# Attention in steps of two units instead of one, with the output products spread anew over the steps

## What is computed

```python
pa, pb, pc, pd = jnp.split(hl @ w_in, COL_SPLITS, axis=-1)
oa = window_attention_sink(qa, ka, va, kac, vac, a_sink, scale64)
ob = dense_attention(qb, cat(kbc, kb), cat(vbc, vb), scale_b)
oc = diff_combine(dense_attention(qc, cat(kcc, kc), cat(vcc, vc), scale_c), c_lambda, c_subln, layer)
od = dense_attention(qd, cat(kdc, kd), cat(vdc, vd), scale64)
out_lat = jnp.concatenate([merge_heads(oa), merge_heads(ob), oc, merge_heads(od)], axis=-1) @ w_out
```

## Time and profile before

| | |
|---|---|
| median of 3 runs | 2156.08 us (2155.17 to 2156.92) |
| the profiled execution, span | 2157.7 us |
| TensorE matmul busy | 1970.7 us, 91% of the span |
| VectorE busy | 676.9 us, 31% |
| ScalarE busy | 529.7 us, 25% |
| GpSimd busy | 156.9 us, 7% |

### The profile page before, as it was taken

The page is one execution under the profiler, slowest core; times in us unless marked ns, Lnnn a source line. Parts: engine busy times, 40 slices in busy tenths (PEclk is TensorE's granted clock), DMA queues, the critical chain, the costliest instruction groups (busy, mean ns, idle before and its releaser), DMA issues. The chain is left out here.

```text
span 2157.7 us, 27259 instructions
## 1 busy us (share of the span) xinstructions
PE 1970.7 (91%) x10878; PEld 931.5 (43%) x10878; DVE 676.9 (31%) x1753; ACT 529.7 (25%) x1220; POOL 156.9 (7%) x155
## 2 busy tenths in 40 slices
PE   5999989999979999999999899889996898887875
PEld 2436465555633332323323556465554333333322
DVE  3322345666650100101001632366666011110203
ACT  3211154565531000100100321166553010000001
POOL 1100010000010010020100201100000000000000
PEclk8999979999989999999999999999998899999998
DMA  9742020000189999999999302110008899999995
GB/s 352 287 161 81 0 79 1 1 2 1 40 322 414 425 365 418 380 391 419 363 414 420 137 20 78 23 57 1 1 1 342 361 427 426 427 426 427 427 427 213
DMA packets 90935, 515.66 MB, mean 239 GB/s; under 512 B 10594, under 2 KB 15628, under 8 KB 36540
## 3 DMA queue, kind: packets, MB, share of 16 engines
q1 hardware_dynamic: 84496, 493.29, 56.4%
q0 software_dynamic: 4416, 15.21, 2.4%
q10 hardware_dynamic: 1900, 5.43, 0.6%
HBM read 498.69 MB, written 15.20 MB: 238 GB/s over the span
## 5 line engine op out<-in xcount | busy, mean ns | idle before, releaser
L712 PE MATMUL psS<-arena 128*64 128x512 f32 (+9 forms) x4552 | 1136.0, 556 | 70.8 <-DMA arena<-in_w_up 23.1
L712 PEld LDWEIGHTS psS<-arena 128*64 128x64 f32 (+4 forms) x4552 | 450.0, 158 | 666.2 <-issue 585.1
L715 PE MATMUL psT<-ident,arena 128*128 128x128 f32 (+1 forms) x1036 | 171.6, 289 | 47.3 <-DVE arena L2053 13.2
L1930 DVE TENSOR_REDUCE mx<-psS 128x1 f32<-128x768 f32 (+2 forms) x200 | 165.5, 827 | 152.1 <-PE psS L712 150.4
L1281 ACT ACTIVATE arena<-psT 128x768 f32<-128x768 f32 (+7 forms) x261 | 150.3, 577 | 244.0 <-PE psT L715 230.3
L1281 ACT ACTIVATE arena<-psS 128x128 f32<-128x128 f32 (+5 forms) x158 | 61.8, 421 | 572.1 <-PE psS L712 527.9
L2106 DVE TENSOR_TENSOR arena<-arena,psS 128x512 f32<-128x512 f32 x32 | 20.5, 684 | 549.6 <-PE psS L712 549.6
L715 PEld LDWEIGHTS psT<-ident,arena 128*128 128x128 f32 (+1 forms) x1036 | 119.5, 144 | 147.3 <-issue 107.9
L712 PE MATMUL psT<-arena 128*32 128x512 f32 x1536 | 174.5, 595 | 0.0
L1281 ACT ACTIVATE arena<-psS,nb 128x768 f32<-128x768 f32 (+2 forms) x200 | 158.1, 794 | 1.4
L712 PE MATMUL psM<-arena 128*128 128x512 f32 x288 | 140.1, 608 | 0.0
(11 more groups left out here) (223 smaller groups left out, 1285.5 us busy)
## 6 DMA issues: line engine op xcount, KB each, us to landing
arena<-in_w_gate SPq DMA_DIRECT2D x117, 1024.0 KB, 12.7
arena<-in_w_up SPq DMA_DIRECT2D x116, 1024.0 KB, 18.2
arena<-in_w_down SPq DMA_DIRECT2D x116, 1024.0 KB, 17.7
arena<-in_w_mod SPq DMA_DIRECT2D x48, 1024.0 KB, 7.4
arena<-in_w_in SPq DMA_DIRECT2D x6, 2048.0 KB, 7.8
arena<-in_w_out SPq DMA_DIRECT2D x8, 512.0 KB, 7.7
arena<-in_w_out SPq DMA_DIRECT2D x2, 2048.0 KB, 15.1
normed_rows<-arena ACTq DMA_DIRECT2D x8, 512.0 KB, 8.1
```

The costliest lines, as they stand in the source:

```text
L712: return nc.tensor.matmul(o, lhsT, rhs, start=start, stop=stop)
L715: return nc.tensor.transpose(o, in_, ident[0:n, 0:n])
L1930: link(V.reduce_max(mx[:, par:par + 1], view(S, 0, P, 0, (512, 2), (1, n)), axis=AX.XY))
```

## The change

Steps now hold a pair of units: 8 steps for a tile instead of 16. Step `s` scores pair `s`, turns pair `s - 1` and multiplies pair `s - 2` by values. On TensorE both score blocks stand at the head of the step (in C, whose units take both `psS` tensors each, the second one stands further back), then the first turn, the values, the early pieces, the second turn, the late pieces and the turn of queries. The reciprocals and the mixing move: VectorE does those of the pair before right after the step's first maximum, and in C mixes the first unit of the pair between the pair's units. `norm_end` comes at the end of the next step's maxima. The output pieces are split into early and late ones and distributed anew; query turns, gate rows and biases have new places. `tail_steps` takes both steps without scores. "open" waits for one more sum. Lists of tiles may now be in another order (`STREAMS`, `min`, `max`); for the lists in use they give what they gave.

```diff
-LAG = 2
-T_AT = 2
-Q_AT = {4: "A", 5: "B0", 6: "B1", 12: "D", 14: "C1"}
-GATE_AT = ((7, 9, 11, 13), (9, 11))
-BIAS_AT = ((3, 5), (7,))
-O_COUNT = {3: 1, 4: 2, 5: 2, 6: 1, 7: 2, 8: 1, 9: 3, 10: 1, 11: 3}
+GROUPS = TURNS // 2
+DIFFERENTIAL = (4, 5)
+T_AT = 1
+Q_AT = {2: "A", 3: "B0", 4: "B1", 5: "D", 6: "C1"}
+EARLY_GATE, LATE_GATE = 0, 1
+GATE_AT = (((3, LATE_GATE), (4, EARLY_GATE), (4, LATE_GATE), (5, EARLY_GATE)), ((4, EARLY_GATE), (5, EARLY_GATE)))
+BIAS_AT = ((1, 2), (3,))
+O_COUNT = {2: (0, 2), 3: (0, 1), 4: (2, 3), 5: (2, 3), 6: (0, 1), 7: (0, 2)}
...
+        t, v = s - 1, s - 2
+        plan.append(Step(s if s < n else None, t if 0 <= t < n else None, v if v >= 0 else None, turns, early, late))
...
-                    before = {8: 7, 12: 14, 13: 15}.get(u, UNIT_SLOTS[u - 1][-1] if 8 < u < 12 else LAST_SLOT[u] - 2)
                     if i or u >= 2:
-                        pe.wait_ge(z["P"], i * SLOTS + before + 1)
+                        pe.wait_ge(z["P"], i * SLOTS + LAST_SLOT[u] - 2 + 1)
...
+                for n, step in enumerate(PLANS[l]):
+                    pair, apart = step.scored, differential(step.scored)
+                    if pair:
+                        scores(2 * pair)
+                    if pair is not None and not apart:
+                        scores(2 * pair + 1)
+                    if step.turned is not None:
+                        turned_probabilities(n, 2 * step.turned)
+                    if step.valued is not None:
+                        values(step.valued)
+                    gate_rows((n, EARLY_GATE))
+                    for x in step.early:
+                        output_piece(*x)
+                    if apart:
+                        scores(2 * pair + 1)
+                    if step.turned is not None:
+                        turned_probabilities(n, 2 * step.turned + 1)
+                    if n in BIAS_AT[l]:
+                        router_bias(BIAS_AT[l].index(n))
+                    gate_rows((n, LATE_GATE))
+                    for x in step.late:
+                        output_piece(*x)
+                    for x in step.turns:
+                        turn(*x, values=2 * step.turned + 1)
+                    if step.valued is not None and step.valued % GROUPS == DIFFERENTIAL[-1]:
+                        turned_back(step.valued)
...
+                            pe.wait_ge(z["oe"], 2 * halves_through(l, n_tiles - 2, 1))
                             pe.sem_inc(z["open"], 1)
...
+                for n, step in enumerate(PLANS[l]):
+                    pair, apart = step.scored, differential(step.scored)
+                    if pair is not None and not apart:
+                        exponentials(2 * pair)
+                    if step.turned is not None:
+                        probabilities_out(2 * step.turned)
+                    if pair is not None:
+                        exponentials(2 * pair + (not apart))
+                    gate_out((n, EARLY_GATE))
+                    if step.turned is not None:
+                        probabilities_out(2 * step.turned + 1)
+                    if apart:
+                        exponentials(2 * pair + 1)
+                    if step.valued is not None and step.valued % 2:
...
+                        a_(ar[:, o:o + 256], bank(6, w=256)).then_inc(z["Oc"], 1)
...
+                for n, step in enumerate(PLANS[l]):
+                    pair, apart = step.scored, differential(step.scored)
+                    units = () if pair is None else (2 * pair,) if apart else (2 * pair, 2 * pair + 1)
+                    slots = [(s, slot) for s in units for slot in UNIT_SLOTS[s % TURNS]]
+                    for s, slot in slots[:1]:
+                        maxima(s, slot)
+                    after_scores(step.turned)
+                    for s, slot in slots[1:]:
+                        maxima(s, slot)
+                    if apart:
+                        mixed(2 * pair)
+                        for slot in UNIT_SLOTS[(2 * pair + 1) % TURNS]:
+                            maxima(2 * pair + 1, slot)
+                    if n - 1 in NORM:
+                        norm_end()
...
```

More of the change, by code:

```diff
@@ L1 @@
+import dataclasses
 import math
@@ L122, in output_pieces, with differential @@
 def output_pieces(at):
-    n = sum(O_COUNT.get(x, 0) for x in range(at))
-    return [divmod(m, KD) for m in range(n, n + O_COUNT.get(at, 0))]
-def attention_plan(tiles):
[L130 to L133, removed]
+    n = sum(sum(O_COUNT.get(x, ())) for x in range(at))
+    early, late = O_COUNT.get(at, (0, 0))
+    pieces = [divmod(n + m, KD) for m in range(early + late)]
+    return pieces[:early], pieces[early:]
+@dataclasses.dataclass
+class Step:
+    scored: "int | None"
+    turned: "int | None"
+    valued: "int | None"
+    turns: list
+    early: list
+    late: list
+def attention_plan(tiles):
+    n, plan = len(tiles) * GROUPS, []
+    for s in range(n + 2):
+        i, at = divmod(s, GROUPS)
+        turns, early, late = [], [], []
+        if s < n and i and at == T_AT:
+            turns.append(("T", i - 1, None))
         if s < n and i + 1 < len(tiles) and at in Q_AT:
             turns.append(("Q", i + 1, Q_AT[at]))
-        if s < n and i and at == T_AT:
-            turns.append(("T", i - 1, None))
         if s < n and i:
[L139 to L142, removed]
-    return plan
+            early, late = ([(i - 1, r, k) for r, k in pieces] for pieces in output_pieces(at))
+        t, v = s - 1, s - 2
+        plan.append(Step(s if s < n else None, t if 0 <= t < n else None, v if v >= 0 else None, turns, early, late))
+    return plan
+def differential(pair):
+    return pair is not None and pair % GROUPS in DIFFERENTIAL
 def tail_steps(plan, early):
-    steps = [n for n, entry in enumerate(plan) if entry[0] is None][1:]
+    steps = [n for n, step in enumerate(plan) if step.scored is None]
     return {step: n for n, step in enumerate(steps[:early])}
 def norm_steps(plan):
-    return {n: entry[2] // TURNS for n, entry in enumerate(plan) if entry[2] is not None and entry[2] % TURNS == 12}
+    return {n: step.valued // GROUPS for n, step in enumerate(plan) if step.valued is not None and step.valued % GROUPS == 6}
 def uses_act(sec, t):
@@ L224, in turns_through @@
 def turns_through(plan, turn):
-    order = [("Q", 0, name) for name in Q_FIRST] + [x for entry in plan for x in entry[3]]
+    order = [("Q", 0, name) for name in Q_FIRST] + [x for step in plan for x in step.turns]
     last = max(i for _, i, _ in order)
@@ L464, in backbone_program @@
         block = ctx.enter_context(nc.Block())
-        PLANS = [attention_plan(list(range(TT))), attention_plan(list(range(TC, TT)))]
         TILES = [list(range(TT)), list(range(TC, TT))]
+        PLANS = [attention_plan(tiles) for tiles in TILES]
+        STREAMS = [sorted(tiles) for tiles in TILES]
         NCONST = 4 + 4 * L
@@ new lines, in turned_back, with gate_rows @@
+                def turned_back(pair):
+                    i = pair // GROUPS
+                    pe.wait_ge(z["Oc"], shared_groups(l, i, 2))
+                    for c in range(2):
+                        a = QN + tiles[i] * QNW + (4 + c) * P
+                        last = tr(psO[:, (2 + c) * P:(3 + c) * P], ar[:, a:a + P])
+                    last.then_inc(z["Cf"], 1)
+                def gate_rows(at):
+                    if at in GATE_AT[l]:
+                        n = GATE_AT[l].index(at)
@@ new lines, in reciprocals @@
+                def reciprocals(pair):
+                    i, c = divmod(pair, GROUPS)
+                    slot = LAST_SLOT[2 * c]
+                    p0 = i % 2 * SLOTS + slot
+                    dve.wait_ge(z["P"], i * SLOTS + slot + 2)
+                    if slot < 4:
+                        e = i % 2 * 4 + slot
+                        link(V.tensor_tensor(rs[:, p0:p0 + 2], rs[:, p0:p0 + 2], esk[:, e:e + 2], ALU.add))
+                    V.reciprocal(rr[:, p0:p0 + 2], rs[:, p0:p0 + 2]).then_inc(z["rr"], 1)
```

280 lines of the change are left out of this document (129 added, 151 removed).

## The result

The changed kernel takes 2178.12 us (median of 4 runs, 2176.88 to 2180.76) against 2156.5 us (4 runs on the same chip, 2155.17 to 2159.96): ratio 1.0109, 95% interval 1.0096 to 1.0123. It is slower by 1.1%, where 0.34% was forecast. The sign was right; the size lies beyond the range of 2152 to 2173 us.

What follows compares the result with a forecast made beforehand. TensorE's order was taken to bound the kernel (91% busy), the chain in group C running level. Terms +5.6 - 1.2 + 3.6 + 2.9 - 3.5 = +7.4 us gave 2165.1 profiled, 2163.5 us as median (0.34% slower), range 2152 to 2173.

Steps and rivals of the forecast that it cites:

- The walk through a full tile: Steps 0 to 7 of a full attention tile, priced from the profile: 59.9 us against 58.45.
- The balance of its terms: In a full tile, 5.0 us of waits where there were 2.2, less 1.4 of trips: +1.4 us.
- the waits before: TensorE's waits in a full tile of the kernel before the change, put at 2.2 us.
- a second turn waiting for a copy that stands third in a chain: TensorE's second turn waits for ScalarE's first-turn copy, behind maximum and exponential; waits of 0.85 and 0.65 in steps 0, 1.
- The saving on trips: In A and D, neighbouring row-split score blocks save one 0.35 us trip in each of 4 pairs: 1.4 us a full tile.
- The first rival: Copies land before TensorE wants them in steps 0, 1 and 6, so trips alone remain: -7 us, 2149 us; faster 0.17.
- The other tiles: Last tiles -1.2 us together, layer 1's first latent +3.6, first context +2.9, second context -3.5, layer 0's first latent 0.
- The step that failed: A fall of TensorE's clock was left out of the sum because the longest wait in full tiles is 1.3 us.
- the clock was made a rival: Half clock in C and D steps of two tiles without pieces and second context tile's pieces: 6 to 10 us, 2171; chance 0.14.
- the forecast's +7.4: Sum over all attention tiles: +5.6 full, -1.2 last, +3.6 and 0 first latent, +2.9 and -3.5 context, in us.

Runs made afterwards that it cites:

- copies first: Changed kernel with ScalarE's two copies of turned probabilities each ahead of the exponential they stood behind, outside C: 2176.76 us, 1.0096 against the kernel before.
- first copy first: Changed kernel with ScalarE's first copy ahead of the first exponential, the second exponential still ahead of the second copy: 2171.61 us, 1.0072 against the kernel before.
- sum later: Changed kernel with VectorE's sum of the last output half moved from the end of step 0 to the end of step 1: 2177.99 us, 1.0114 against before.
- pieces in A: Changed kernel with the edit of mixing behind and three real product pieces moved from steps 2, 3 and 4 to 0 and 1: 2160.62 us, 1.0018 against before.
- scores parted: Changed kernel with TensorE's second score block of a pair behind the first turn, in A, B and D: 2177.33 us, 1.0097 against the kernel before.
- mixing behind: Changed kernel where, in C, VectorE mixes the former unit behind all maxima of the new one: 2172.43 us, 1.0067 against the kernel before.

## Why the size was off

*The walk through a full tile* came out at 60.28 for 59.9, each step within 0.25 us, six waits of 4.7 us for the 5.0 forecast. The balance of its terms was 0.4 short for another reason: the waits before, which it put at 2.2 us a tile, are 1.8 by the trace (58.45 less 56.6 busy). What it named as the cause, a second turn waiting for a copy that stands third in a chain, is what the timeline shows; copies first, first copy first and sum later add that the chain runs through two steps at a time, so that no one copy in it is the cause.

*The saving on trips*, 4 x 0.35 = 1.4 us a tile, is the term whose account was wrong. A trip is worth 0.21 us in D and 0.42 in A, 1.2 us of TensorE's busy time a tile, so the price was about right; but in all four steps that have one a wait for ScalarE's copy stands behind it, and putting the trips back cost 0.07 us a tile. The walk held in spite of it, since in a step with such a wait the copy's time counts, and not what TensorE saved ahead of it. The first rival (2149 us) rested on these trips alone and had nothing under it.

*The other tiles* (changed against forecast): first latent tile of layer 1 +6.8 for +3.6, first context tile +4.5 for +2.9, second −4.5 for −3.5, first latent tile of layer 0 +4.1 for 0. Of the +6.8, some 2.8 are step 2 at 8.81 us, which is 6.04 with pieces in A and in sum later; the other 4.0 are the 3.6 forecast. Of the +4.1, 2.9 are step 2 at half clock. The first context tile's length hangs on the clock from one execution to the next: 43.7 in the profiled execution, 38.4 us in sum later, whose code differs in nothing there before its second tile, 43.9 with scores parted. One execution of each kernel therefore doesn't test the +2.9 for it. The two last tiles gave −0.5 for −1.2, and what isn't attention −1.4.

*The step that failed* is the one by which the clock was made a rival with a chance of 0.14 and put at nothing in the sum, "against it: in the full tiles the longest wait is 1.3 us". The longest single wait is 1.20 us, as forecast, and the clock fell all the same, in a B step behind steps 0 and 1, in which TensorE waits three times. In the profiled execution this cost 2.9 + 2.8 + 1.7 = 7.4 us in three tiles, and the forecast's +7.4 with it makes 14.8 of the 17.9; 0.4 more in each of four full tiles makes 16.4, and the rest, +1.5, is the balance of the other tiles' errors, in which 1.3 us more of clock are hidden. That rival's 2171 us was priced at the C and D steps of the two sparse tiles and the second context tile's pieces. It had a part of the place right. The D steps of the first context tile, in the changed kernel and in sum later:

```profile
306.90:316.24 9.34, 7.61 (x45) 0.63 0.00 0
301.87:309.96 8.09, 5.17 (x44) 1.00 0.00 1
```

The larger bills lie in B steps, which it left out, one of them in a full tile. The second context tile's clock did not fall at all: it stood at 1.00 after and at 0.92 before.

That something to do in steps 0 and 1 keeps the clock up in step 2 is shown by the count above, 15 of 32 tiles without, 0 of 20 with; the medians, 4.9 and 5.2 us shorter with steps 0 and 1 together as long as before, agree with it and would not carry it alone. How much of the 21.6 us between the medians is clock can't be read from them; single executions of one program span 2167 to 2183 us (sum later), at a mean granted clock of 0.976 in the shortest and 0.969 in the longest. Nor is the clock a matter of the change alone: over the whole span the two profiled executions stood at 0.971 before and 0.972 after. What decides in which tile it falls stays open. In mixing behind, two neighbouring full tiles have the same steps 0 and 1 (5.81 and 6.63 us), and step 2 takes 7.22 us in one and 8.92 in the other. The Trainium skill (TensorE: Matmul & The Clock Gate, Part 1) calls the number of slow matmuls at a kernel's start "run-variable"; the traces here show the like for falls in the middle of a kernel.

*The steady part of the loss*: 1.8 us a full tile. The mixing ahead of the second maximum is 0.6 of it, shown. The remaining 1.3 come back when three pieces are put into the waits of steps 0 and 1. So in a full tile the pair step with the pieces laid out for it is level with the kernel before; the layout and the place of the mixing cost the time. Where a tile has no pieces, the pair step keeps its price: in the first latent tile of layer 1 4.0 us with the 2.8 of step 2 taken off, 5.3 in pieces in A, of which 1.5 is its last D step (7.81 us where the changed kernel has 6.32). No version that was run beats the kernel before; the best is slower by 0.2% (interval 0.02 to 0.34%).

## What to carry to other kernels

When two units of work are put into one step, walk the relay between engines once through the step, look for the waits at its end, and put independent work there before judging the change; reordering the engine that the wait names mostly moved the wait to the next step here. A saving on an engine's own instructions counts only where no wait for another engine stands behind it in the step. Where a change adds waits, price a fall of the clock into the sum even if each wait is short, and look for its bill in the dense step behind them.

## What the runs showed of the hardware

Needless matmuls made a kernel shorter: with two products in each of six tiles the median was 4.9 us lower. The granted clock stayed at 1.00 (2.4 GHz) in the B step behind them in all 8 tiles counted, where without them it was 0.70 and 0.81 over the step, in part at 1.2 GHz, in two of the changed kernel's four; a B pair's eight score matmuls took 5.33 us at the lower level and 2.75 at the higher. Score blocks that split the array by rows cost 0.85 us each apart and 1.49 (D) or 1.28 (A) for two side by side. And the same program's executions differ by up to 16 us (2167.15 to 2183.39), while its steps at full clock repeat to 0.02 us; the clock has a part in that, 1.7 to 2.9 us in a tile where a trace shows it, and that it is all of it isn't shown.
